# Conv taps, gates and GDN's pairs laid beside other work, RWKV's old state kept by VectorE, and half of the filler products taken out

## What is computed

```
def step(state, inp):                                   # RWKV-7, per token
    sa = einsum('bhij,bhj->bhi', state, a_t)
    state = state * w_t + sa[..., None] * b_t + v_t[..., None] * k_t
    return state, einsum('bhij,bhj->bhi', state, r_t)

qkv = silu(causal_depthwise_conv(qkv, conv_w))          # GDN, width 4
q, k = l2norm(q) * 128 ** -0.5, l2norm(k)
decay = exp(where(causal, gc[..., :, None] - gc[..., None, :], -inf))
amat  = where(strict, (k * beta) @ k.T * decay, 0)      # solved per chunk of 64
qk    = q @ k.T * decay
state = state * g_last + k_dec.T @ v_new                # per chunk
o = rmsnorm(o, norm_g) * silu(gate)
```

## Time and profile before

| | us |
|---|---|
| median of 3 runs | 3651.26 |
| lowest and highest | 3646.37, 3656.15 |
| the profiled execution | 3646.52 |
| its span, first to last instruction | 3644.5 |

### The profile page before, as it was taken

The page is one execution under the profiler, slowest core; times in us unless marked ns, Lnnn a source line. Parts: engine busy times, 40 slices in busy tenths (PEclk is TensorE's granted clock), DMA queues, the critical chain, the costliest instruction groups (busy, mean ns, idle before and its releaser), DMA issues. The chain is left out here.

```text
span 3644.5 us, 46484 instructions
## 1 busy us (share of the span) xinstructions
PE 3281.0 (90%) x18528; PEld 2627.4 (72%) x18528; DVE 2234.5 (61%) x3550; ACT 1316.6 (36%) x1872; POOL 631.2 (17%) x606
## 2 busy tenths in 40 slices
PE   8997889998997898998986888889999997899998
PEld 7874578886883577886754775767787797777787
DVE  7888657995768657995646664544533425644524
ACT  2234535773233535773212012132132325632222
POOL 0036320001016410002402221111000104411000
PEclk9987789999997888999998988989999999999999
DMA  7620006992620005991220000022222221122222
GB/s 285 260 93 1 6 13 244 375 352 88 236 90 1 1 21 203 374 375 64 93 87 1 2 2 1 2 75 81 93 93 93 81 93 38 44 99 81 93 95 78
DMA packets 59591, 401.40 MB, mean 110 GB/s; under 512 B 6768, under 2 KB 8432, under 8 KB 12272
## 3 DMA queue, kind: packets, MB, share of 16 engines
q1 hardware_dynamic: 53616, 356.49, 27.0%
q0 software_dynamic: 5760, 41.95, 3.1%
HBM read 396.31 MB, written 2.10 MB: 109 GB/s over the span
## 5 line engine op out<-in xcount | busy, mean ns | idle before, releaser
L141 PE MATMUL ps<-t_part,weight_hi 128*128 128x512 f32 x2152 | 862.9, 401 | 69.6 <-DVE scr_part L186 38.2
L143 PE MATMUL ps<-t_part,ring_lo 128*128 128x512 f32 x2152 | 848.9, 394 | 0.0
L142 PE MATMUL ps<-scr_part,weight_hi 128*128 128x512 f32 x1640 | 648.7, 396 | 0.0
L141 PEld LDWEIGHTS ps<-t_part,weight_hi 128*128 128x128 f32 x2152 | 412.6, 192 | 164.0 <-DVE ring_lo L173 69.3
L351 DVE TENSOR_TENSOR ring_lo<-ring,weight_hi 128x2048 fp32r<-128x2048 f32 x133 | 315.3, 2370 | 340.6 <-ACT weight_hi L344 340.6
L344 ACT CAST weight_hi<-ring 128x2048 fp32r<-128x2048 f32 x133 | 253.8, 1908 | 668.3 <-PE ps L143 668.3
L143 PEld LDWEIGHTS ps<-t_part,ring_lo 128*128 128x128 f32 x2152 | 411.3, 191 | 87.7
L142 PEld LDWEIGHTS ps<-scr_part,weight_hi 128*128 128x128 f32 x1640 | 315.3, 192 | 70.0 <-issue 5.1
L142 PE MATMUL ps<-big_part,weight_hi 128*128 128x512 f32 x512 | 200.9, 392 | 0.0
L3210 DVE SCALAR_TENSOR_TENSOR big<-ps,rstd 128x512 f32<-128x512 f32 x64 | 44.2, 690 | 164.1 <-PE ps L143 163.9
L207 POOL TENSOR_TENSOR big<-big 128x512 f32<-128x512 f32 x28 | 47.8, 1707 | 549.1 <-ACT big L200 545.6
(11 more groups left out here) (655 smaller groups left out, 6958.2 us busy)
## 6 DMA issues: line engine op xcount, KB each, us to landing
ring<-in_w_moe SPq DMA_DIRECT2D x84, 1024.0 KB, 5.1
t<-in_w_moe SPq DMA_DIRECT2D x84, 1024.0 KB, 5.1
ring<-in_w SPq DMA_DIRECT2D x64, 1024.0 KB, 4.9
t<-in_w_ada POOLq DMA_DIRECT2D x40, 1024.0 KB, 6.7
ring<-in_w_in SPq DMA_DIRECT2D x32, 1024.0 KB, 6.3
ring<-in_even_in SPq DMA_DIRECT2D x15, 1024.0 KB, 4.9
ring<-in_qkv SPq DMA_DIRECT2D x12, 1024.0 KB, 4.9
ring<-in_w_out SPq DMA_DIRECT2D x8, 1024.0 KB, 4.9
```

What stands on the lines that cost most here:

```text
L141: pe.matmul(bank, w_hi, x_hi, start=first, stop=False)
L142: pe.matmul(bank, w_hi, x_lo, start=False, stop=False)
L143: return pe.matmul(bank, w_lo, x_hi, start=False, stop=last)
```

## The change

Eight edits.

1. **Filler.** `keep_busy` goes from TotalBeside (2), mlstm_opening (2 and 3), scatter_tokens (2), gdn_pairs (2 after each of three heads), and with their stages from gdn_conv (6) and gdn_scale_tokens (5). It stays in the norms, rwkv_mix, rwkv_decays, mlstm's end and the end of rwkv_scan.
2. **Old state.** The identity product is gone. VectorE holds `decayed(p)`, the state times its next decay, and the update is sum times decay plus that, written block by block on the diagonal (two 64x64 operations per pair). After it VectorE makes the next `decayed`. The decays are no longer stored times 64.
3. **Conv beside the scan.** In group 1's scan VectorE makes one tap of tiles 22 and 23 per chunk, ScalarE their sigmoids, GpSimd the products at the end. The stage gdn_conv is gone.
4. **Pairs.** Head h uses banks (5h + i) % 8, and X and E have two buffers each. TensorE may make the rows of head h+1 as soon as head h-1 is done, and VectorE the argument of head h+1 right after the product with -1 of head h.
5. **Tokens.** Turning and scaling are one stage; k is scaled out of PSUM by VectorE, v by ScalarE.
6. **Gates.** The four silu of the gate are made beside gdn_scan, by ScalarE and GpSimd.
7. **Gate stage.** One product per tile instead of a sigmoid and two.
8. The waits between VectorE's operations at the end of a head are fewer.

```
 def pe_(pe):                                           # rwkv_scan
-                pe.matmul(o, K.ident[:, :], state(c, p), start=True, stop=False)
-                pe.matmul(o, btok[:, t, hd], U(c)[:, hd], start=False, stop=False)
+                pe.matmul(o, btok[:, t, hd], U(c)[:, hd], start=True, stop=False)
                 pe.matmul(o, ktok[:, t, hd], V(c)[:, hd], start=False, stop=True).then_inc(sr.up(), 1)
...
 def v_(v):
+        for p in range(2):
+            v.memset(decayed(p), 0.0).then_inc(st.up(), 1)
-        v.memset(K.scr[:, 7424:7680], 0.0).then_inc(sc.up(), 1)
+        v.memset(K.scr[:, 7424:7936], 0.0).then_inc(sc.up(), 1)
...
+            if conv:
+                conv_tap(v, c)
...
-                v.scalar_tensor_tensor(out=state(c + 1, p), in0=K.ps[:, p, 0:P],
-                                       scalar=K.pc[:, 2 * grp + p, c:c + 1], in1=K.bd[:, :],
-                                       op0=ALU.mult, op1=ALU.mult).then_inc(sc.up(), 1)
+                v.wait_ge(st.sem, st.n)
+                for q in HALVES:
+                    v.scalar_tensor_tensor(out=state(c + 1, p)[q, q], in0=K.ps[q, p, q],
+                                           scalar=K.pc[q, 2 * grp + p, c:c + 1], in1=decayed(p)[q, q],
+                                           op0=ALU.mult, op1=ALU.add).then_inc(...)
+            for p in range(2 if c + 1 < NC else 0):
+                v.wait_ge(st.sem, st.n)
+                v.wait_ge(sc.sem, sc.at(2 * c + p + 2))
+                v.tensor_scalar(decayed(p), state(c + 1, p), K.pc[:, 2 * grp + p, c + 1:c + 2], None, ALU.mult).then_inc(st.up(), 1)
...
 def pe_(pe):                                           # gdn_pairs
         for h in range(4):
-            if h >= 1:
-                pe.wait_ge(cl.sem, cl.at(h))
+            if h >= 2:
+                pe.wait_ge(cl.sem, cl.at(h - 1))
...
+            if h >= 1:
+                pe.wait_ge(bs.sem, bs.at(h))
             for t in range(ST):
...
-            keep_busy(K, pe, 2 if h < 3 else 0)
```

More of the change, by code:

```diff
@@ L1828, in conv_beside, with gated @@
     return taps, sigmoid, rest
[L1831 to L1836, removed]
-    def v_(v):
[L1839 to L1873, removed]
-            v.wait_ge(sg.sem, sg.at(i + 1))
-            if silu:
-                v.tensor_tensor(G(i), G(i), g, ALU.mult).then_inc(K.sig("v_step").up(), 1)
-                v.wait_ge(K.sig("v_step").sem, K.sig("v_step").n)
-            v.tensor_tensor(o, y, G(i), ALU.mult).then_inc(us.up(), 1)
-    K.stage(name, scalar=s_, vector=v_)
+def gated(K, name, pairs):
+    def v_(v):
+        for y, g in pairs:
+            v.tensor_tensor(y, y, g, ALU.mult).then_inc(K.sig("v_step").up(), 1)
+    K.stage(name, vector=v_)
 def route(K, hT, Pm, Pm_t, const, group_of, w_src, moe):
@@ L2682, in rwkv_scan, with conv_tap, s_ @@
     half = lambda c: slice(64 * (c % 2), 64 * (c % 2) + 64)
+    decayed = lambda p: (K.scr_p[:, :], K.scr_p2[:, :])[p]
+    conv = (K.big(22), K.big(23)) if grp else ()
+    summed, gate = K.sig("conv_sum"), K.sig("conv_sigmoid")
+    CA, CG = (lambda i: K.big(29 + i)), (lambda i: (K.big(31), K.work[:, :])[i])
+    def conv_tap(v, n):
+        i, j = n // 4, 3 - n % 4
+        d, w = 3 - j, cw[:, 12 * j + 10 + i:12 * j + 11 + i]
+        if j == 3:
+            v.tensor_scalar(CA(i), conv[i], w, None, ALU.mult).then_inc(st.up(), 1)
+            return
+        v.wait_ge(st.sem, st.n)
+        v.scalar_tensor_tensor(out=CA(i)[:, d:S], in0=conv[i][:, 0:S - d], scalar=w, in1=CA(i)[:, d:S],
+                               op0=ALU.mult, op1=ALU.add).then_inc((st if j else summed).up(), 1)
+    def s_(s):
+        for i in range(len(conv)):
+            s.wait_ge(summed.sem, summed.at(i + 1))
+            s.activation(CG(i), CA(i), ACT.Sigmoid).then_inc(gate.up(), 1)
     def pe_(pe):
@@ L2735, in g_ @@
             g.tensor_copy(V(c)[half(c), :], vtok[half(c), c // 2, 256 * grp:256 * (grp + 1)]).then_inc(vc.up(), 1)
+        if conv:
+            g.wait_ge(vc.sem, vc.at(NC))
+        for i in range(len(conv)):
+            g.wait_ge(gate.sem, gate.at(i + 1))
+            g.tensor_tensor(conv[i], CA(i), CG(i), ALU.mult).then_inc(K.sig("g_step").up(), 1)
     def v_(v):
@@ L2802, in v_, with argue @@
+        def argue(h):
+            v.wait_ge(ar.sem, ar.at(h + 1))
+            v.tensor_tensor(X(h), mats(h, 0), K.tri[:, 1:2, :].to_broadcast([P, 4, P]), ALU.add).then_inc(argument.up(), 1)
+        argue(0)
         for h in range(4):
+            v.wait_ge(ex.sem, ex.at(ST * (h + 1)))
             v.wait_ge(sp_.sem, sp_.at(h + 1))
-            v.tensor_tensor(X, bank(0), K.tri[:, 1:2, :].to_broadcast([P, 4, P]), ALU.add).then_inc(ar.up(), 1)
-            v.wait_ge(ex.sem, ex.at(ST * (h + 1)))
@@ L2914, in v_, with s_, g_ @@
             v.wait_ge(st.sem, st.n)
-    K.stage("gdn_scan", tensor=pe_, vector=v_)
+    sigmoid = K.sig("gate_sigmoid")
+    def s_(s):
+        for x, y in gates:
+            s.activation(y, x, ACT.Sigmoid).then_inc(sigmoid.up(), 1)
+    def g_(g):
+        for i, (x, y) in enumerate(gates):
+            g.wait_ge(sigmoid.sem, sigmoid.at(i + 1))
+            g.tensor_tensor(y, y, x, ALU.mult).then_inc(K.sig("g_step").up(), 1)
+    K.stage("gdn_scan", tensor=pe_, vector=v_, scalar=s_, gpsimd=g_)
 EVEN_ROWS = 1
```

110 lines of the change are left out of this document (62 added, 48 removed).

## The result

| | before | after |
|---|---|---|
| median, us | 3651.46 (4 runs) | 3616.28 (4 runs) |
| lowest and highest | 3646.37, 3656.15 | 3614.42, 3621.78 |
| the profiled execution | 3646.52 | 3614.42 |
| its span, mean granted clock | 3644.5, 0.925 | 3612.6, 0.924 |

The ratio of after to before is 0.9906, with a 95% interval from 0.9889 to 0.9924: 35 us faster by the medians, 32 by the two spans. The forecast was 3621, between 3604 and 3639. In a later set of runs the same two programs gave 3616.86 and 3653.82, ratio 0.9897 (0.9882 to 0.9912).

The account below looks back on a forecast made before the run. TensorE, busy 90% of the span, bounds the scan; barriers, table loads or engines waiting in turn bound most other changed stages. Terms sum to -29.6 us: 3646.52 to 3617, plus 4.7 for a median, 3621; range 3604 to 3639.

Parts of the forecast that it names:

- Scans: Both RWKV scans: 3.5 us gained in group 0, 2.8 in group 1, about 0.5 lost per head; -5.2 us.
- Conv stage: Stage ahead of gdn_q_and_k: 8.1 us go, slower q and k squares cost 2.4 (0 to 6.4); -5.7 us.
- Pairs: gdn_pairs: next head's exponentials run during this head's weighing; 23.5 us of 30.5, -7 us (-5.5 to -9.5).
- Tokens: Turning and scaling merged: -5.1 us, +1.4 for gdn_scan's first chunk at half clock; -3.7 us.
- the gate: Gate stage: table load gone, four products follow the barrier and end near 2382.7; -4.8 us.
- Inverse: GDN's inverse, behind the pairs: no change counted in the sum; one rival had it +26 us.
- (d): Rival, slower: mlstm twice and GDN's inverse stay at 1.2 GHz throughout; sum +16 us, 3667; chance 0.04.
- Filler of the first block: mlstm_opening: -2.3 us, +1.1 for clock (-2 to +5) per layer, -2.4; ends of w_out and scatter_tokens -0.8.
- The forecast for a median: Whole kernel: 4.7 us added to 3617, since the median of runs lay that much above the profiled execution; 3621.
- (c): Rival: VectorE bounds the new scan, a round of 4.7 us again, dropped products save nothing; 3627, chance 0.08.
- (a): Rival: clock suffers more in squares, pairs, gdn_scan, mlstm and the scans' start; -13 us, about 3638, chance 0.20.
- (b): Rival: kind clock, pairs at 21 us, squares and scan at 2.4 GHz, mlstm earlier warm; -41, 3610, chance 0.10.

Follow-up runs that it names:

- the repeat: The changed kernel once more, without any edit: 3616.86 us, ratio to before 0.9897.
- opening_only: The kernel before with the filler of mlstm_opening alone taken out: 3644.00 us, ratio to before 0.9975.
- state_only: The kernel before with VectorE keeping the old state in both scans, no conv tap, gdn_conv still a stage: 3642.61 us, ratio to before 0.9971.
- filler_back: The changed kernel with filler restored in mlstm_opening, TotalBeside and scatter_tokens, not in gdn_pairs: 3626.77 us, ratio to before 0.9927.
- head_filler: The changed kernel with one filler product at the head of each norm that subtracts no mean: 3619.76 us, ratio to before 0.9911.
- rows_ahead: The changed kernel with TensorE making head 1's rows ahead of head 0's products in gdn_pairs: 3617.77 us, ratio to before 0.9903.

## Why the prediction was right

The time came out 4.7 us below the forecast and inside the range. That it came so close is in part luck. The terms of the change miss by 6.4 us together (-36.0 measured for -29.6), and the two stretches that it does not touch, +2.3 and +1.8, take most of that back. By its own steps:

- **Scans, -5.2 predicted, -6.6 measured** (-3.3 and -3.1 in the scans, -0.2 between them; the repeat has -2.6 and -3.1). The working held: a chunk of 4.25 for 4.26, the head 0.55 dearer for 0.5, four updates in 1.23 for 1.2. In group 1 I spread a loss of 0.1 per chunk over all; it was 0.65, most of it from GpSimd's product in one chunk, which I had counted as free because the two products "come after its last copy", without asking whom they run beside. What I left out was on the other side: the first chunk runs at half clock and gained 0.7, not 0.44, and before's group 1 had begun with a slower head (3.14 us, 2.68 in group 0). The terms as they stand there add up to -5.3, not -5.2.
- **Conv stage, -5.7 predicted, -5.3 measured.** 7.6 gone (8.1, less 0.5 by which the spreads of rwkv_norm ahead of it came later), the squares +1.4 where I took +2.4, and +1.0 in the spreads, which I had not priced: the low clock did not stop at the squares.
- **Pairs, -7 predicted, -6.7 measured** (-6.6 to -8.0 in the six profiles of this gdn_pairs in the changed kernel's surroundings, -5.2 alone in before's). What bounds it is as told: VectorE from head 1 on, and a TensorE at 1.2 GHz ahead of it. The bound of -5.5 did not reach far enough for the stage by itself.
- **Tokens, -5.1 + 1.4 predicted, -5.3 + 0.5 measured**, and the gate, **-4.8 and -5.0**. The durations of the earlier trace rows carried over. The 0.5 is TensorE's clock in the first chunk of gdn_scan, 0.60 for 0.85.
- **Inverse, 0 predicted, -1.1 measured.** Rival (d) feared it slow; it got faster. The clock had fallen 5 us before the stage began and not with it, so it was back at 1.00 after 4.9 us, for 10.6 in before. The first 10 us of the stage or so (in before from 1.3 us behind its start), granted clock 0.54 in before, then 0.76 in after:

```profile
2270.00:2280.00 10.00, 8.80 (x171) 8.45 (x171) 4.76 (x10) 1.12 (x3) 5.43 (x8) 0.54 0.01 2
```

```profile
2246.00:2256.00 10.00, 7.55 (x188) 7.09 (x190) 5.06 (x11) 1.12 (x3) 6.63 (x9) 0.76 0.01 2
```

- **Filler of the first block, -2.4 - 0.8 predicted, -6.5 in the first comparison.** This is the term that was mis-sized. By the profiles' means it is -3.5 for the openings and mLSTM; by the timed runs of opening_only -9.1 (-5.8 to -12.4). The start itself came out as priced: -2.2 + 0.95 for -2.3 + 1.1, the same in all nine profiles. What the value has at nothing is the clock in the rest of mLSTM (the start and it together had -2 to +5 around +1.1; layer 0 shows 0.95 - 4.0 = -3.1): -4.0 in layer 0 and +1.6 in layer 1 in the first comparison, -1.4 to -4.1 and +1.5 to +1.7 over the nine, against kernels with the filler that move as far by themselves (0 to -4.2, and 0 to +3.2).
- **The forecast for a median**: I added the 4.7 us by which the median lay over before's profile. After's median lies 1.9 over its own profile, so this put 2.8 us of the 4.7 on the forecast; the other 1.9 is the sum of the terms, -31.9 for -29.6, and rounding. The other medians of before, 3651.3 to 3654.2, place its first profile 5 to 8 us under the usual time: the two spans understate the gain, and the 35 to 37 us of the medians are the better figure.

Of the rivals, (c), VectorE bounds the new scan, is refuted by state_only and the waits for TensorE in group 0; (a) and (d) asked for a clock that drops over mLSTM and the inverse, and it did not. (b), the kind clock, asked for squares at full speed and pairs of 21 us; they took 8.79 us, 7.28 before, and 23.8. The filler still in place matters for (a): taking it too brought 11 us of loss.

## What to carry to other kernels

A stretch that waits on barriers, table loads and engines in series can be priced within a microsecond from the durations of its own rows; one whose TensorE clock sits between the two levels cannot, and two profiles of one program differ there by up to 5 us in a stretch, so take a second profile of both kernels before explaining such a difference. Here filler paid where TensorE would stand idle inside a norm and real products follow, and cost where it outlasted the work ahead of a barrier; judge it place by place with timed runs. When a reordering shortens a stage, look whether other profiles of the old order did so too. When an operation is given to an idle GpSimd, look at which VectorE operations run beside it.

## What the runs showed that I had not expected

- A stage that hangs on the clock can have a few fixed lengths, not a spread: mLSTM of layer 0 took 43.6 to 43.8, 44.6 to 44.8, 46.4 or 47.6 to 47.8 us over fourteen profiles, the first and the last of these with the same code of that stage and its opening (filler_back and before).
- TensorE's filler can arrive cold: 2.04 us for two records ahead of q's squares, and then it is no cover but a delay.
- A saving can be the clock's and not the edit's: gdn_pairs with one and the same code was up to 1.3 us shorter in a kernel changed elsewhere (head_filler), as much as in rows_ahead, and in both most of it came back in the inverse.
- One VectorE multiplication took 0.61 us instead of 0.29 beside one GpSimd product, and this made a chunk 0.46 us longer; the half updates beside the same product, which read PSUM, were not held.
